# The gate rows of four mLSTM heads: spread over 128 partitions by DMA through DRAM instead of by TensorE products

## The reference, cut to what matters

```python
def mlstm_chunk(carry, inp):
    C, n, m = carry
    q, k, v, ig, lf = inp
    b = jnp.cumsum(lf, axis=-1)
    logw = jnp.where(causal, b[..., :, None] - b[..., None, :] + ig[..., None, :], -jnp.inf)
    log_prev = b + m[..., None]
    m_t = jnp.maximum(log_prev, jnp.max(logw, axis=-1))
    w = jnp.exp(logw - m_t[..., None])
    a = jnp.exp(log_prev - m_t)
    s = jnp.einsum('bhtd,bhsd->bhts', q, k) * w
    num = a[..., None] * jnp.einsum('bhtd,bhde->bhte', q, C) + jnp.einsum('bhts,bhse->bhte', s, v)
    ...
```

## Time and profile before

| | us |
|---|---|
| median of 3 runs | 1074.53 |
| lowest and highest run | 1074.39, 1075.54 |
| the profiled execution, its own time | 1074.62 |
| its span, first to last instruction | 1072.9 |
| PE busy in the span | 1057.4 (99%) |
| DVE, ACT, POOL busy | 689.7, 465.1, 220.3 |

### The profile page before, as it was taken

The page is one execution under the profiler, slowest core; times in us unless marked ns, Lnnn a source line. Parts: engine busy times, 40 slices in busy tenths (PEclk is TensorE's granted clock), DMA queues, the critical chain, the costliest instruction groups (busy, mean ns, idle before and its releaser), DMA issues.

```text
span 1072.9 us, 20465 instructions
## 1 busy us (share of the span) xinstructions
PE 1057.4 (99%) x8428; PEld 1052.9 (98%) x8428; DVE 689.7 (64%) x1142; ACT 465.1 (43%) x813; POOL 220.3 (21%) x182
## 2 busy tenths in 40 slices
PE   7999999999999999999999999999999999999997
PEld 6999999999999999999999999999999999999997
DVE  6987752357866676555655556598875235877544
ACT  7466641246662245333322223446664124666323
POOL 2442100022201220210332222244310002220111
PEclk9999999999999999999999999999999999999998
DMA  7489572388833366445454225547958337983322
GB/s 223 90 184 199 108 184 87 101 162 173 174 85 97 63 129 122 70 57 75 74 78 69 72 65 73 139 89 169 205 109 186 90 92 155 180 179 63 109 72 84
DMA packets 245061, 127.00 MB, mean 118 GB/s; under 512 B 9088, under 2 KB 243624, under 8 KB 244840
## 3 DMA queue, kind: packets, MB, share of 16 engines
q1 hardware_dynamic: 206952, 106.81, 41.2%
q0 software_dynamic: 38016, 18.88, 14.3%
HBM read 122.38 MB, written 3.28 MB: 117 GB/s over the span
## 4 chain that ended last, share of the span: by engine, by line
PE 97%; ACT 1%; DMA 1%; DVE 0%; SPq 0%; issue 0%; POOL 0%; ACTq 0%
PE dense L565 55%; PE dense L664 30%; PE core_banks L664 5%; PE core_banks L800 1%; PE core_banks L815 1%; PE core_banks L818 1%; PE core_banks L790 1%; PE core_banks L565 1%; PE dense L714 1%; DMA x_tok<-in_x_prompt 1%; PE core_banks L784 0%; PE core_banks L827 0%; PE core_banks L786 0%; PE core_banks L701 0%; PE core_banks L601 0%
## 5 line engine op out<-in xcount | busy, mean ns | idle before, releaser
L1293 DVE TENSOR_TENSOR w_lo<-w_raw,w_hi 128x1024 fp32r<-128x1024 f32 (+2 forms) x119 | 131.6, 1124 | 55.4 <-ACT w_hi L945 55.3
L565 PE MATMUL dense<-xg_hi,w_hi 128*128 128x272 f32 x768 | 162.5, 293 | 1.7 <-DVE xg_lo L1298 1.7
L565 PE MATMUL dense<-xg_lo,w_hi 128*128 128x272 f32 x768 | 158.8, 288 | 0.0
L565 PE MATMUL dense<-xg_hi,w_lo 128*128 128x272 f32 x768 | 158.8, 288 | 0.0
L945 ACT ACTIVATE w_hi<-w_raw 128x1024 fp32r<-128x1024 f32 (+2 forms) x120 | 107.2, 907 | 96.3 <-PE dense L565 82.4
L565 PE MATMUL dense<-h_hi,w_hi 128*128 128x272 f32 x684 | 142.5, 290 | 0.0
L565 PE MATMUL dense<-h_lo,w_hi 128*128 128x272 f32 x684 | 141.3, 288 | 0.0
L565 PE MATMUL dense<-h_hi,w_lo 128*128 128x272 f32 x684 | 141.1, 287 | 0.0
L664 PE MATMUL dense<-x_op_hi,w_lo 128*128 128x272 f32 x432 | 124.8, 289 | 0.0
L664 PE MATMUL dense<-x_op_hi,w_hi 128*128 128x272 f32 x432 | 124.8, 289 | 0.0
L664 PE MATMUL dense<-x_late_hi,w_hi 128*128 128x272 f32 x432 | 124.7, 289 | 0.0
(11 more groups left out here) (299 smaller groups left out, 2146.5 us busy)
## 6 DMA issues: line engine op xcount, KB each, us to landing
w_src<-in_w_ffn_gate SPq DMA_DIRECT2D x90, 256.0 KB, 4.5
w_raw<-in_w_ffn_up SPq DMA_DIRECT2D x90, 256.0 KB, 3.6
w_raw<-in_w_in SPq DMA_DIRECT2D x32, 512.0 KB, 8.4
w_raw<-in_w_ffn_down SPq DMA_DIRECT2D x32, 384.0 KB, 3.9
w_raw<-in_w_ffn_down SPq DMA_DIRECT2D x32, 320.0 KB, 3.5
w_src<-in_w_ffn_gate POOLq DMA_DIRECT2D x36, 256.0 KB, 5.7
w_raw<-in_w_ffn_up POOLq DMA_DIRECT2D x36, 256.0 KB, 5.6
w_raw<-in_w_ffn_gate SPq DMA_DIRECT2D x8, 512.0 KB, 5.7
```

The source lines that it names most:

```text
L565: last = nc.tensor.matmul(out[:, half, 0:TH], w[:, s % 4, k, :], x(kt)[:, half * TH:(half + 1) * TH], start=start and n == 0 and m == 0, s ...
L1293: nc.vector.tensor_tensor(w_lo[:, s % 4, 0:nk, :], w_raw[:, s % RAW, 0:nk, :], w_hi[:, s % 4, 0:nk, :].bitcast(F32), ALU.subtract).then_in ...
```

## The change

The row products go: `step_rows`, `sel_r`, `bm_split`, and the three small ACT and DVE instructions that fed them. POOL now spreads the rows with DMAs. `spread_rows(0)` waits for `gate_rows_ready`, writes the four rows to a scratch tensor `row_copy` in DRAM, waits for that to land, and issues a DMA that reads row 0 for each of the 128 partitions into `row_all[:, 0]` (128 x 544 float32, 272 KB). `spread_rows(1)` does the same for row 1 into the other half. Those for heads 2 and 3 are issued at u = 3 of heads 0 and 1, after `arg_ready` and `past_ready` of the head whose half they take. DVE's `step_arg` and ACT's `past` read `row_all` in SBUF. PE's `step_scores` no longer waits for `past_ready`; for head 0 it waits for `gate_cols_ready` instead. ACT, in head 0 at u = 2, makes its gate column copies first and the `split_hi` after them. What `gate_columns` does is as it was.

```diff
+        row_all = sb("row_all", [P, 2, T])
+        row_copy = nc.dram_tensor("row_copy", (H, T), F32, kind="Internal").ap()
...
             def step_scores(h):
-                if h < H:
-                    pe.wait_ge(evicted, T_IN + 4 * h + 3)
-                    pe.wait_ge(past_ready, h + 1)
-                else:
+                if h >= H:
                     pe.wait_ge(rotated, 2 * (h - H) + 2)
-                    pe.wait_ge(evicted, T_IN + 4 * h + 3)
+                pe.wait_ge(evicted, T_IN + 4 * h + 3)
+                if h:
                     pe.wait_ge(normed, h)
                     pe.wait_ge(normed_act, h)
+                else:
+                    pe.wait_ge(gate_cols_ready, 1)
...
-            def step_rows(h):
-                if h == 0:
-                    pe.wait_ge(gate_cols_ready, 1)
-                    pe.wait_ge(bm_split_ready, 1)
-                else:
-                    pe.wait_ge(normed, h)
-                    pe.wait_ge(normed_act, h)
-                for out, cols in ((X[:, 2, :], slice(0, TP)), (X[:, 3, 0:TS], slice(TP, T))):
-                    nc.tensor.matmul(out, sel_r[:, h, :], bm_split[:, 0, cols], start=True, stop=False)
-                    last = nc.tensor.matmul(out, sel_r[:, h, :], bm_split[:, 1, cols], start=False, stop=True)
-                last.then_inc(rows_spread, 1)
...
-                    elif u == 3:
-                        early = 1 if h else 4
-                        product(s, bank_of(t), *xg, range(early), True, False)
-                        if h:
-                            step_turn(h - 1)
-                        if h < H:
-                            step_rows(h)
-                        product(s, bank_of(t), *xg, range(early, DT), False, True).then_inc(unit_done, 1)
+                    elif h and u == 3:
+                        product(s, bank_of(t), *xg, range(1), True, False)
+                        step_turn(h - 1)
+                        product(s, bank_of(t), *xg, range(1, DT), False, True).then_inc(unit_done, 1)
...
-                    source = X[:, 2, CH[c]] if c < NC else X[:, 3, 0:TS]
-                    last = nc.scalar.activation(past[:, CH[c]], source, ACT.Exp, bias=m_prev_all[:, h, c:c + 1])
+                    last = nc.scalar.activation(past[:, CH[c]], row_all[:, h % 2, CH[c]], ACT.Exp, bias=m_prev_all[:, h, c:c + 1])
...
-                        nc.scalar.activation(bm_split[:, 0, :], rows[:, BM_ROW, :], ACT.Copy).then_inc(bm_hi_ready, 1)
-                        nc.scalar.activation(sel_r[:, :, :], sel[:, :, :], ACT.Copy)
...
-                        nc.vector.tensor_tensor(bm_split[:, 1, :], rows[:, BM_ROW, :], bm_split[:, 0, :].bitcast(F32),
-                                                ALU.subtract).then_inc(bm_split_ready, 1)
...
             def step_arg(h):
-                dve.wait_ge(rows_spread, h + 1)
+                dve.wait_ge(rows_spread[h % 2], 16 * (h // 2 + 1))
...
-                nc.vector.tensor_tensor(grid(weights_arg[:, 0:TP]), grid(X[:, 2, :]), m, ALU.add)
+                nc.vector.tensor_tensor(grid(weights_arg[:, 0:TP]), grid(row_all[:, h % 2, 0:TP]), m, ALU.add)
...
+            def spread_rows(h):
+                if h == 0:
+                    pool.wait_ge(gate_rows_ready, 1)
+                    nc.gpsimd.dma_start(row_copy[:, :], rows[:, BM_ROW, :]).then_inc(rows_copied, 16)
+                    pool.wait_ge(rows_copied, 16)
+                if h >= 2:
+                    pool.wait_ge(arg_ready, h - 1)
+                    pool.wait_ge(past_ready, h - 1)
+                nc.gpsimd.dma_start(row_all[:, h % 2, :], row_copy[h:h + 1, :].broadcast_to([P, T])).then_inc(rows_spread[h % 2], 16)
+
+            spread_rows(0)
+            spread_rows(1)
             for h in range(2 * H):
                 for u in range(4):
+                    if h < 2 and u == 3:
+                        spread_rows(h + 2)
```

More of the change, by code:

```diff
@@ L219, in hybrid_trunk_step @@
         table = sb("table", [P, tables.shape[1]])
-        sel_r = sb("sel_r", [H, H, P], F32R)
-        bm_split = sb("bm_split", [H, 2, T], F32R)
+        row_all = sb("row_all", [P, 2, T])
         state_in = sb("state_in", [P, 2 * H, V1])
@@ L352, in hybrid_trunk_step @@
         state_loaded = sem("state_loaded")
-        bm_hi_ready = sem("bm_hi_ready")
-        bm_split_ready = sem("bm_split_ready")
         gates_biased = sem("gates_biased")
@@ L361, in hybrid_trunk_step @@
         rotated = sem("rotated")
-        rows_spread = sem("rows_spread")
+        rows_spread = [sem(f"rows_spread{n}") for n in range(2)]
+        rows_copied = sem("rows_copied")
         arg_ready = sem("arg_ready")
@@ L1236, in _ @@
                 for u in range(4):
-                    if h or u:
+                    if h or u in (1, 3):
                         split_hi(0, U_IN + 4 * h + u + 2, 0)
@@ L1243, in _ @@
                     if h == 0 and u == 2:
-                        act.wait_ge(gate_rows_ready, 1)
-                        nc.scalar.activation(bm_split[:, 0, :], rows[:, BM_ROW, :], ACT.Copy).then_inc(bm_hi_ready, 1)
                         act.wait_ge(mixer_consts, 1)
-                        nc.scalar.activation(sel_r[:, :, :], sel[:, :, :], ACT.Copy)
                         act.wait_ge(gate_cols_moved, 1)
@@ L1256, in _ @@
                         act.wait_ge(gate_cols_ready, 1)
+                        split_hi(0, U_IN + 4 * h + u + 2, 0)
                     if u == 2 and h < H:
@@ L1795, in step_arg @@
                 m = mask[:, :].rearrange("p (c d) -> p c d", c=1).broadcast_to([P, NC, P])
-                nc.vector.tensor_tensor(grid(weights_arg[:, 0:TP]), grid(X[:, 2, :]), m, ALU.add)
-                nc.vector.tensor_tensor(weights_arg[0:TS, TP:T], X[0:TS, 3, 0:TS], mask[0:TS, 0:TS], ALU.add).then_inc(arg_ready, 1)
+                nc.vector.tensor_tensor(grid(weights_arg[:, 0:TP]), grid(row_all[:, h % 2, 0:TP]), m, ALU.add)
+                nc.vector.tensor_tensor(weights_arg[0:TS, TP:T], row_all[0:TS, h % 2, TP:T], mask[0:TS, 0:TS], ALU.add).then_inc(arg_ready, 1)
             split_lo(0, U_IN + 1, 0)
@@ L1819, in _ @@
                         gate_rows_end()
-                    if h == 0 and u == 1:
-                        dve.wait_ge(bm_hi_ready, 1)
-                        nc.vector.tensor_tensor(bm_split[:, 1, :], rows[:, BM_ROW, :], bm_split[:, 0, :].bitcast(F32),
-                                                ALU.subtract).then_inc(bm_split_ready, 1)
                     if u == 3:
```

## The result

The changed kernel takes 1077.98 us (median of 7 runs, 1076.66 to 1079.1) against 1074.39 for the kernel before on the same chip: a ratio of 1.0029, with an interval of 1.0018 to 1.0041. It is slower by 0.3%, where 1070.1 was forecast. Twelve more runs, beside the last experiment, give 1078.18 and 1.0027 [1.0017, 1.0038]. The profiled execution took 1077.11 us, 2.49 more than the 1074.62 of the profiled execution before.

The account below looks back on a forecast made before the run. PE, busy 99% of the span, was taken as the bound. Savings of 4 x 0.97 + 0.65 = 4.53 us off 1074.62, with the new transfers costing nothing, gave 1070.09; range 1069.6 to 1072.9.

Parts of the forecast that it names:

- Row products, heads 1 to 3: From the turn to the third dense pair PE takes 1.05 us instead of 2.02, saving 0.97 a head, 2.91 in three.
- rival E: Another engine is the bound in heads 1 to 3, so PE gives nothing there: 1073.0 us, chance 0.03.
- Head 0's products and the wait for `past`: In head 0 PE saves 0.97 us of row products and 0.65 by no longer waiting for ACT's `past`.
- Who waits, and from when: PE waits at head 0's updates, 8.42 us after DVE's `step_arg` begins; the row is free up to 417.74.
- The new transfers, head 0: Write to DRAM 3.5 us, spreading 5.4; row there at 417.72, bounds 416.3 to 422.9, at no cost to PE.
- rival A: Head 0's row lands between 418.2 and 420.0, PE waits up to 2.3 us at the updates: 1071.3, chance 0.25.
- The price of a microsecond of lateness: At head 0's updates, each microsecond the row comes after 417.74 costs PE one.
- POOL's issue: POOL takes 1.28 us to issue a DMA.
- Heads 1 to 3's transfers: Rows for heads 1 to 3 take at worst 8.4 us, are used much later, and cost nothing.
- C: Head 0's row is late by the upper bounds, at 422.9; PE waits 5.2 us: 1075.2, middle 1074, chance 0.11.
- D: Head 0's write queues 9.7 us behind weight transfers, spreading takes 8.4; PE waits 9.2 us: 1079.3, chance 0.03.
- B: DVE's splits hold up POOL's DMAs by 0.98 us each in head 0; PE waits 1.94: 1072.0, chance 0.10.

Follow-up runs that it names:

- the last experiment: The changed kernel with only SP's load of head 2's u = 0 weights held until row 0 has landed: 1071.47 us, ratio 0.9967.
- The experiment on heads 1 to 3: The kernel before with rows of heads 1 to 3 spread by DMA and head 0's still by TensorE products: 1071.53 us, ratio 0.9971.
- the quiet kernel: The changed kernel with head 1's u = 2 weights held until row 0 landed, table and retention states loaded after head 1's weights: 1069.72 us, ratio 0.9954.
- the kernel with the hold alone: The changed kernel with SP holding head 1's u = 2 and 3 weights until row 0 has landed, table and states unmoved: 1070.01 us, ratio 0.9962.

## Why the prediction was wrong, point by point

**Row products, heads 1 to 3: right.** From the turn to the third dense pair it is now 1.05 us, as it was in head 4, against 2.02. PE in head 1:

```profile
449.42 0.60 PE L825 MATMUL core_banks<-sum_ident,o_tok 128*128 128x128 f32 x4
...
450.47 0.42 PE L564 MATMUL dense<-xg_hi,w_lo 128*128 128x272 f32 x2
```

The experiment on heads 1 to 3 gives the same 2.91 in the time, and by that rival E falls.

**Head 0's products and the wait for `past`: right.** The scores begin at 417.92, 0.25 behind the last pair; "about 417.9" was forecast. The 4.53 us as a whole are borne out by the quiet kernel, 4.7 us faster than the kernel before, and by the kernel with the hold alone, 4.6.

**Who waits, and from when: right.** The chain from the argument to the end of DVE's scores takes 431.65 - 423.08 = 8.57 us, for 8.42 in the prediction. The difference is ACT's, whose five `past` now take 1.47 us instead of 1.26. PE stopped at the place that was named, and only there. The row was free up to 417.7 and came 5.4 later, and PE waited 5.4.

**The new transfers, head 0: this step failed.** The prediction took 3.5 for the write and 5.4 for the spreading, and put the row at 417.72. They took 4.9 and 9.0, with 423.08 for DVE's start. The 9.0 lies above even the upper bound of 8.4. The reasoning behind the size was wrong in one sentence: rival A's "POOL has its own queue, in which nothing is ahead". The queue was its own, and SP's loads in another queue held it up all the same. A row that warned of it stood in the prediction: the tiny loads that took 9.7 us, explained away as a matter of SP's own queue. Two further things were missed. The landing times of the earlier trace rows were no estimate for this place, though not because their stretches were quiet: the DMA share in the five microseconds after those issues was 0.62 to 1.30, against the 0.86 of the earlier trace rows. So the share of busy time says little of how long a transfer takes. What differs is what SP has in flight: in the kernel before the mixer's 512 KB loads take 8.4 us to land by the median, and the 256 to 384 KB loads of the FFNs 3.5 to 4.5. That this is the reason is argued; no run varies the size alone. And the change itself bears on the traffic: with the subtraction gone from DVE, SP's next weight load could leave 1.2 us earlier, and it left right in front of the new transfer. The sentence "the loads behind them share the DMA engines" priced what the rows do to the loads, and never what the loads do to the rows.

**The price of a microsecond of lateness: incomplete.** "Each microsecond later costs PE one" left out the clock: by the rows a wait of 5.4 us cost 7.15, one of 2.9 cost 4.5. With it, the row at 423.08 gives 1077.2, without it 1075.5, inside the 0.2% that would have been called no change. So the lateness alone took the gain away, and the clock made it a loss.

**POOL's issue: a small miss.** Each DMA took POOL 0.6 us and not 1.28.

**Heads 1 to 3's transfers: right.** Row 2 took 4.0 us and row 3 8.4, and neither was waited for.

**The rivals.** A's wait of up to 2.3 us was exceeded; what it put against itself, the empty queue, was no protection. C was nearest in number: a row at 422.9 by the upper bounds. It had been given 0.11, and its price of 1075.2 lacked the clock. D named the cause, transfers of weights on the same DMA engines, though with the long part in the write; it was given 0.03. Together they should have stood ahead of the forecast. B falls: DVE's bracket shows it idle for the 9.25 us in which the spreading travelled, and it had ended its last step at 413.83, before POOL issued at 414.01. Only the write, issued at 408.81, fell beside a DVE split, and with the same overlap on quiet DMA engines it took 1.9 us.

On what the pages say of such transfers: the Trainium skill, page "DMA: Bandwidth & Descriptors", section "Anatomy of one DMA — SWDGE (gpsimd) path", fits the time of one such DMA as 2.0 us plus its bytes over 436,000 a microsecond. By that fit the write is estimated at 2.0, and 1.9 was measured on quiet engines; the spreading is estimated at 2.6, and 3.8 was measured. Beside SP's loads the write took 4.0 to 7.8, and right behind them the spreading took 7.0 to 12.4. The same page, section "Queues, rings and completion order", says that each DMA engine takes turns between its queues, a packet at a time. The stretch from 414 to 418 us, with 745 packets of SP's queue and none of POOL's, doesn't look like that, nor does the one with 1093 of SP's and 7 of ACT's. The rows don't tell whether the packets waited at the engines, or at the memory, or hadn't been handed over yet. That SP's transfers delay the row is shown, and where on the way they do is not.

## What to carry to other kernels

A DMA put on the critical path is to be priced by what is in flight when it is issued, on all queues, and the change's own effect on the other queues' issue times counts in that; the same 272 KB took 3.8 us with the engines quiet, 9.0 when a weight load had gone out 0.8 us before it, and 12.4 when a load, the table and the states had. A high share of busy DMA time isn't the measure of it. If such a DMA is worth having, hold the prefetches that aren't urgent behind it: one wait in SP's order turned a loss of 0.3% into a gain of 0.3 to 0.4%, and with the table moved as well 0.5%. And price a wait of PE of some microseconds at more than its length: here 2.9 and 5.4 us cost about 1.7 more each.

## What the runs showed of the hardware

- A POOL DMA of 8.5 KB from SBUF to DRAM landed in 1.9 us on quiet DMA engines (twice), and in 4.0 to 7.8 us beside weight loads (4.0, 4.5, 4.6, 4.9, 5.1, 7.0, 7.8).
- The first broadcast read of 272 KB by POOL took 3.6 to 3.8 us without a weight load right in front (three traces), and 7.0 to 9.5 with one (five traces); then it landed within 0.7 us of that load. In the first 4 us after its issue the changed kernel moved 745 packets of SP's queue and none of POOL's; with ACT issuing, 1093 and 7 in 5 us.
- Of 5.4 us of idling PE spent the last 3 at a granted clock of 0.50, and it worked at 0.50 for some 3.5 us more. After 2.9 us of idling it worked at full clock for 1.2 us and then at 0.50 for 3.4. The cost was 1.77 and 1.6 us.
- Issued from ACT's queue, the same two transfers gave times from 1071.62 to 1079.39 us over ten runs, the widest spread of all kernels here. Its cause is open.
- ACT's exp of 128x544 from SBUF into `past` took 1.47 us, where 1.26 was read with PSUM as the source.
